# Overflow branches nested in a hand-ordered MoE kernel, TensorE's read of the count placed ahead of its last sums, and ScalarE's table loads placed ahead of its waits

## The reference

```
for li in range(DEPTH):
    h = modulate(rmsnorm(x), sh1, sc1)
    mix = even_mixer(h, h_ctx, ...) if li % 2 == 0 else hyena_mixer(h, ...)
    x = x + g1 * mix
    h = modulate(rmsnorm(x), sh2, sc2)
    x = x + g2 * moe(h, ...)

# in s5_mixer                          # in moe
z = jax.nn.gelu(y)                     _, idx = lax.top_k(scores + router_b, TOP_K)
out = z * sigmoid(z @ glu_w + glu_b)   hid = silu(xb @ w_gate[e]) * (xb @ w_up[e])
                                       out = (hid @ w_down[e]) * w
```

## Time and profile before

| | before |
|---|---|
| time, median of 3 executions | 1480.05 us (1479.48 to 1481.05) |
| the profiled execution's own time | 1483.4 us |
| its span in the profile | 1481.6 us |
| PE busy | 1320.5 us, 89% of the span |
| DVE / ACT / POOL busy | 634.6 / 295.5 / 66.5 us |
| mean granted TensorE clock | 0.953 of full speed |
| moved by DMA | 502.76 MB, mean 339 GB/s |
| ACT table loads | 15, of 1283 ns each |

### The profile page before, as it was taken

How to read it: one execution, slowest core, us unless ns; L and a number is a source line. 1 busy time by engine, 2 the same in 40 slices (tenths; PEclk the granted TensorE clock), 3 DMA queues, 4 the chain that set the end, 5 groups by cost and what they waited for, 6 DMA issues and landing times.

```text
span 1481.6 us, 21810 instructions
## 1 busy us (share of the span) xinstructions
PE 1320.5 (89%) x9040; PEld 691.3 (47%) x9040; DVE 634.6 (43%) x1166; ACT 295.5 (20%) x499; POOL 66.5 (4%) x116
## 2 busy tenths in 40 slices
PE   4998778899999979888898999999999988888888
PEld 1444325765444324333346766875444333333333
DVE  5897743263433222232234688644443232232232
ACT  2236332321111111111112113031111111111110
POOL 0000681000000000000000000000000000000000
PEclk9899898999999989999997999989999999999999
DMA  9572972958999999999999772585899999999995
GB/s 382 223 201 73 172 282 87 394 215 330 398 422 422 425 423 430 426 431 426 429 421 311 288 255 100 231 321 203 353 422 422 423 430 426 431 427 428 427 426 236
DMA packets 50582, 502.76 MB, mean 339 GB/s; under 512 B 9324, under 2 KB 16236, under 8 KB 19820
## 3 DMA queue, kind: packets, MB, share of 16 engines
q1 hardware_dynamic: 49932, 499.18, 84.2%
q10 hardware_dynamic: 544, 2.10, 0.3%
HBM read 496.57 MB, written 4.69 MB: 338 GB/s over the span
## 4 chain that ended last, share of the span: by engine, by line
PE 59%; DMA 30%; DVE 5%; issue 2%; ACT 2%; SPq 1%; ACTq 0%; DVEq 0%
PE ps L701 55%; DMA arena<-in_w_experts 25%; DMA arena<-in_ada_w 4%; PE ps L1007 2%; PE ps L425 2%; ACT arena L1318 1%; DVE arena L1931 1%; SPq L469 1%; DVE arena L2107 0%; PE ps L746 0%; ACT L1318 0%; DVE arena L1764 0%; DVE arena L1765 0%; PE ps L954 0%; DVE arena L1762 0%
## 5 line engine op out<-in xcount | busy, mean ns | idle before, releaser
L701 PE MATMUL ps<-arena 128*32 128x512 f32 (+13 forms) x8220 | 1233.9, 488 | 140.9 <-issue 52.6
L701 PEld LDWEIGHTS ps<-arena 128*32 128x32 f32 (+6 forms) x8220 | 628.4, 132 | 732.5 <-issue 594.2
L1318 ACT ACTIVATE arena<-ps 128x512 f32<-128x512 f32 (+7 forms) x303 | 167.3, 552 | 921.1 <-PE ps L701 776.4
L1972 DVE SCALAR_TENSOR_TENSOR arena<-arena,ps 128x256 f32<-128x256 f32 x44 | 21.2, 481 | 244.4 <-ACT arena L1318 244.4
L1318 ACT ACTIVATE arena<-arena 128x256 f32<-128x256 f32 (+7 forms) x136 | 90.8, 694 | 164.9 <-DVE arena L1992 58.3
L1990 DVE CAST arena<-ps 128x512 bf16<-128x512 f32 x42 | 29.1, 692 | 164.9 <-PE ps L701 164.9
L1927 DVE COPY arena<-ps 128x512 f32<-128x512 f32 x44 | 30.4, 692 | 133.8 <-PE ps L701 133.8
L1960 DVE TENSOR_TENSOR arena<-arena 128x1024 bf16<-128x1024 f32 x42 | 51.5, 1226 | 37.3 <-ACT arena L1318 37.0
L691 POOL MEMSET arena<- 128x1 f32 x2 | 0.2, 102 | 1214.5 <-PE ps L1007 1214.5
L1007 PE MATMUL ps<-arena 128*128 128x128 f32 x352 | 52.8, 273 | 0.0
L1992 DVE TENSOR_TENSOR arena<-ps,arena 128x1024 f32<-128x1024 f32 x42 | 51.4, 1225 | 1.4
(11 more groups left out here) (226 smaller groups left out, 488.9 us busy)
## 6 DMA issues: line engine op xcount, KB each, us to landing
arena<-in_w_experts SPq DMA_DIRECT2D x76, 3072.0 KB, 20.8
arena<-in_w_experts SPq DMA_DIRECT2D x52, 2048.0 KB, 19.6
arena<-in_w_experts SPq DMA_DIRECT2D x52, 1024.0 KB, 19.0
arena<-in_ada_w SPq DMA_DIRECT2D x40, 1024.0 KB, 6.1
arena<-in_hy_w_in SPq DMA_DIRECT2D x6, 2048.0 KB, 11.1
arena<-in_ada_w SPq DMA_DIRECT2D x4, 2048.0 KB, 22.5
arena<-in_w_shared SPq DMA_DIRECT2D x2, 3072.0 KB, 10.2
arena<-in_hy_w_out SPq DMA_DIRECT2D x1, 4096.0 KB, 13.0
```

What stands on the lines that cost most here:

```text
L701: return pe.matmul(out, lhsT, rhs, start=start, stop=stop, skip_group_check=skip)
L1318: return act.activation(out, in_, func, **kw)
L1972: stt(hh, sg, wtab[:, n:n + 1], ps[:, GU, FF:2 * FF], M, M).then_inc(sem("h_done"), 1)
```

## The change

Five edits:

1. `overflow` nests its branches: the branch for pass s+1 stands inside the body of pass s. An engine without overflow takes one branch in place of four. The read of the count is a function of its own, `most_tokens`; on PE it is called ahead of the waits for the last sums, on the other engines it stays where it was.
2. A one-element activation on scratch (`f(at(r_pad+2,1), at(r_eps,1), X)`) is put ahead of a wait of ACT in four places: Exp before the softmax loop, Gelu before the wait for `y_mm`, Sigmoid before the wait for `glu_mm`, Sqrt before the wait for the 15th `filter_mm`. The number of table loads stays 15.
3. The copy of `ys` out of PSUM was two copies on DVE; the second is now made by ACT, with a semaphore of its own.
4. `ql_normed` and `kvl_normed` become two counts of one semaphore, `lat_normed`.
5. In `normed`, `folded` is made ahead of the wait for `rms_ready`.

```diff
-        def overflow(li, eng, body):
-            r = eng.value_load(flags[:, li:li + 1], min_val=0, max_val=L + HALF)
-            for s in range(1, L // S + 1):
-                with eng.If(r > s * S):
-                    with eng.Fori(0, NE) as i:
-                        body(s, i)
-                eng.nop()
+        def most_tokens(li, eng):
+            return eng.value_load(flags[:, li:li + 1], min_val=0, max_val=L + HALF)
+
+        def overflow(eng, body, most, s=1):
+            with eng.If(most > s * S):
+                with eng.Fori(0, NE) as i:
+                    body(s, i)
+                if s < L // S:
+                    overflow(eng, body, most, s + 1)
+            eng.nop()
...
-                overflow(li, sp, more)
+                overflow(sp, more, most_tokens(li, sp))
...
-            pe.wait_ge(sem("ql_normed"), 1)
+            pe.wait_ge(sem("lat_normed"), 1)
...
-            pe.wait_ge(sem("kvl_normed"), 1)
+            pe.wait_ge(sem("lat_normed"), 2)
...
             attention_part(5)
-            pe.wait_ge(sem("y_evicted"), 2)
+            pe.wait_ge(sem("y_evicted"), 1)
+            pe.wait_ge(sem("y_evicted_act"), 1)
...
+                most = most_tokens(li, pe)
                 pe.wait_ge(sem("oh_ready"), (li + 1) * NG)
                 pe.wait_ge(sem("y_dve"), 2 * (li + 1) * NG)
                 last_to_tokens((0, 1)).then_inc(sem("sc_mm"), 1)
...
-                overflow(li, pe, more)
+                overflow(pe, more, most)
...
             act.wait_ge(sem("uscr_out"), 16)
+            f(at(r_pad + 2, 1), at(r_eps, 1), ACT.Exp)
             for n in range(2 * HEADS):
...
             turned(act, f, ch, 2 * HEADS - 1)
+            f(at(r_pad + 2, 1), at(r_eps, 1), ACT.Gelu_apprx_tanh)
+            act.wait_ge(sem("y_mm"), 1)
+            ch.then(f(ys.rearrange("p t (q b) c -> p b q t c", b=2)[:, 1], ps[:, 4, :].rearrange("p (q t c) -> p q t c", t=T5, c=C5), ACT.Copy), "y_evicted_act")
             act.wait_ge(sem("yT_mm"), 1)
...
+            f(at(r_pad + 2, 1), at(r_eps, 1), ACT.Sigmoid)
             for j in range(4):
                 act.wait_ge(sem("glu_mm"), j // 2 * 2 + 2)
...
+                    f(at(r_pad + 2, 1), at(r_eps, 1), ACT.Sqrt)
                     act.wait_ge(sem("filter_mm"), 14 + 1)
...
-                dve.wait_ge(sem("rms_ready"), 4 + use)
                 if jsh == 3:
                     ch(tt(folded, ident[:, 0:NE], ident[:, NE:P], AD))
+                dve.wait_ge(sem("rms_ready"), 4 + use)
...
-            for b in range(2):
-                ch.then(dve.tensor_copy(ys.rearrange("p t (q b) c -> p b q t c", b=2)[:, b],
-                                        ps[:, 3 + b, :].rearrange("p (q t c) -> p q t c", t=T5, c=C5)), "y_evicted")
+            ch.then(dve.tensor_copy(ys.rearrange("p t (q b) c -> p b q t c", b=2)[:, 0],
+                                    ps[:, 3, :].rearrange("p (q t c) -> p q t c", t=T5, c=C5)), "y_evicted")
```

More of the change, by code:

```diff
@@ L691, in moe_pool @@
                 pool.memset(ov_pad, 0.0).then_inc(sem(f"ov_t{li}"), 1)
-                overflow(li, pool, more)
+                overflow(pool, more, most_tokens(li, pool))
             moe_pool(0)
@@ L1514, in more @@
                     f(sg[0:S], ps[0:S, GU, 0:FF], ACT.Silu).then_inc(sem(f"ov_a{li}"), 1)
-                overflow(li, act, more)
+                overflow(act, more, most_tokens(li, act))
             moe_act(0)
@@ L1728, in _ @@
             ch(stt(ql[:, 0], ql[:, 0], col("qn", 0), rsx[:, 0:L], M, M))
-            ch.then(stt(ql[:, 1], ql[:, 1], col("qn", 1), rsx[:, 0:L], M, M), "ql_normed")
+            ch.then(stt(ql[:, 1], ql[:, 1], col("qn", 1), rsx[:, 0:L], M, M), "lat_normed")
             dve.wait_ge(sem("rms_ready"), 3)
             ch(dve.reciprocal(stx, stx))
-            ch.then(stt(kvl, kvl, col("kvn"), stx, M, M), "kvl_normed")
+            ch.then(stt(kvl, kvl, col("kvn"), stx, M, M), "lat_normed")
             for i in range(16, CTAB_STEPS):
@@ L2028, in more @@
                     dve.wait_ge(ovp, i * OVP + OVP * base + 6)
-                overflow(li, dve, more)
+                overflow(dve, more, most_tokens(li, dve))
                 for j in range(KD):
```

## The result

| | before | after |
|---|---|---|
| first measurement, median of 5 | 1480.05 us | 1471.59 us (1469.80 to 1474.18) |
| the profiled execution, time / span | 1483.4 / 1481.6 us | 1474.18 / 1472.3 us |
| mean granted clock in the profile | 0.953 | 0.961 |

The ratio is 0.9946, 95% interval [0.9926, 0.9965]: 8.0 us faster by it, 8.5 by the medians, where 4.95 was forecast and 1472.4 was the low end of the range. So the range was missed by 0.8 us. A second measurement gave a median of 1472.49 us, just inside it, and a ratio of 0.9950 [0.9930, 0.9970].

The account below looks back on a forecast made before the run. The prediction took PE to bound the kernel, with 59% of the chain (DMA 30%); -1.25 - 1.6 - 1.3 - 0.3 - 0.5 = -4.95 us from the median of 1480.05 gave 1475.1 us, range 1472.4 to 1478.9.

Parts of the forecast that it names:

- The end of MoE 0: PE's overflow branch in layer 0 comes 1.6 us earlier, its stall stays 5.74 us, token norms start earlier: -1.25 us.
- the queue-bound rival: Layer 0's stall came from asking at a bad moment; asked earlier it costs 3.3 us: -3.5 for -1.25, 1472.8 us, chance 0.15.
- The moved read: PE's read of the count, 0.8 us, ahead of the last sums: taken as hidden, otherwise costing 0.8 us in each layer.
- the rival on the slow side: One jump brings one fetch more, so PE stops twice in each layer: 1480 to 1482.4 us, chance 0.12.
- The gelu: Behind PE's part of attention, ACT's table is already loaded and the gelu begins right away: -1.3 us.
- Exp and Sigmoid: Earlier table loads at the softmax and the gate give 0, since PE waits for weights and DVE for PE; Exp's bound -0.5.
- The folded table: Between ACT's mean square and the reciprocal, 0.24 us moves ahead of an idle DVE wait in both layers: -0.5 us.
- The kernel's end: SyncE's final 1.8 us wait for PE goes, less 0.2 for rounding and the meeting itself: -1.6 us.
- PE drops out, the whole wait goes: At the kernel's end, one jump finishes by 1476.4 or 1478.7, before SyncE is ready at some 1479.7; its 1.8 us wait vanishes.
- The sqrt: At Hyena's filter norms, the table load comes forward at most 0.45 us within PE's 1.79 us wait: -0.3 us.

Follow-up runs that it names:

- one_body: The changed kernel with TensorE's four overflow bodies written as one loop of 256 rounds, so PE jumps over some 124 instructions; ratio 0.9947 to the kernel before.
- its halves: Two kernels against the one before: the overflow part alone, ratio 0.9979, and everything but the overflow part, ratio 0.9982.
- nest_load: The kernel before with the overflow part alone (nested branches, PE's read of the count ahead of the last sums); ratio 0.9979 to the kernel before.

## Why the prediction fell short

The direction and the places were right, the size was not: 8.5 us by the first medians, 8.4 by the means, for 4.95, and below the range. By its steps:

- *The end of MoE 0, -1.25*: measured -1.31, -1.40 and -1.42 in three profiles. The stall kept its length within 0.6 us, one fetch stayed, and the queue-bound rival (a stall of 3.3 us) did not occur. The moved read was hidden: the sums follow each other as before. The rule of the Trainium skill, "Runtime: NRT & Kernel Launch", section "Instruction fetch mechanics", that a taken branch beyond the window of two pages waits for a fetch, agrees with one_body (no stall over one body, 3.4 to 6.5 us over four). A second stall, the rival on the slow side, came in no kernel with nested branches.
- *The gelu, -1.3*: -1.26. The row was right against the 2.7 that the Trainium skill, "ScalarE: Activation LUTs", section "What ACT_TABLE_LOAD costs", would give: ScalarE's next activation follows the load at once.
- *Exp and Sigmoid, 0*: as forecast, shown for Exp by the longer wait for the weights, and for Sigmoid by the lead of the changed kernel, 3.3 us before and behind the gate. Ahead of the weights the Exp gave more than the 0.5 us put as its bound.
- *The folded table, -0.5*: gone from the path in both layers; but in layer 1 the wait for `in_mcst` took it and 1 us more; the sum had no term for what else could be late there.
- *The kernel's end, -1.6, mis-sized*: 0.7 between the first profiles, and 0.2 in the mean of four profiles with the old branches (5.93, 4.56, 6.13 and 4.95 us from the start of PE's last matmul to the end) against the changed kernel's (5.26 and 5.17). All seven with branches one behind another have a mean of 5.47 us, all nine with nested ones 5.31. The step "PE drops out, the whole wait goes" took the output's own 2.3 us as fixed, and took the first profile for the rule.
- *The sqrt, -0.3, the step that failed*: PE's idle time was priced as time alone, and the clock behind it put at nothing without a reason. The gap itself shrank by the 0.34 us forecast. But the clock goes with it: with both the gap shorter and the overflow edit in, 6.8 us at 1.2 GHz became 0 to 3.4 and 10.2 became 6.8, which is 1.4 and 1.7 us of the first two spans' difference. In the times the sqrt's edit is worth 2.8 us (0.8) on top of the overflow part, and the whole change 2.3 us (1.1) more than its halves.

With the clock taken out by the regression the change is worth 4.6 us (error 0.5), against a sum of 4.95. That agreement is partly luck: the end was put 0.9 to 1.4 too high, the wait for `in_mcst` was not foreseen, and the places of the profile give 2.9. What stays open is the rest of the surplus. Three microseconds of the difference of the first two spans are chance (the stretch from 233 to 243 us, and that at 291 us, which is as short in nest_load as in the changed kernel). Why the read ahead, worth 1 us in its profile, is worth 3.2 in the times, and why a filled gap gives 3 us in each profile and 1.2 in the times, isn't settled; nor is what decides between none, 3.4 and 6.8 us behind the same gap. Each kernel has one or two profiles, and the timed executions show their mean clock but not where it was low.

## What to carry to other kernels

Where PE stands idle for one or two microseconds between long busy stretches, read the granted clock behind the gap before pricing it: filling a gap of 1.8 us was worth 3.0 us in the profile, though only 1.2 (0.5) in the times. A jump over code is priced by its distance, so keep what is jumped over small, or loop in it; and where a fetch moves, look which transfer it will meet. A stage that starts earlier may find its data not there yet, as in one_body behind the token norms and in the changed kernel at MoE 1. Compare two profiles of one kernel before explaining a difference of a few microseconds between two kernels.

## What was not expected of the hardware

- A gap of PE of 1.79 us, in four profiles, and one of 1.45, in two of eight, came with 6.8 us at 1.2 GHz, begun 0.7 to 0.9 us ahead of its end; with the gap filled there was none in six profiles out of six.
- Where a block of PE's instructions (16 KB) came in beside the last of the output, the output was there 4.7 to 5.2 us after PE's last matmul began, in nine profiles, against 3.8 to 4.2 in five without; four others do not fit.
- PE's jump over some 496 instructions stalled 3.4 to 6.5 us in every profile; a jump over some 124 took 0.2 to 0.4 us in most places and 1.1 to 5.8 in one or two of the four at the end of each layer.
